# A two-block transformer kernel on one core: where ScalarE's function tables are asked for, and which set serves logarithm and exponential

## Time and profile before

| | |
|---|---|
| median of 3 runs | 3647.27 us (3642.99 to 3649.27) |
| the profiled execution | 3647.55 us |
| its span, first to last instruction | 3645.8 us |
| instructions | 48080 |
| mean granted TensorE clock | 0.92 of full |
| transfers | 325.77 MB, mean 89 GB/s |

### The profile page before, as it was taken

The page is one execution under the profiler, slowest core; times in us unless marked ns, Lnnn a source line. Parts: engine busy times, 40 slices in busy tenths (PEclk is TensorE's granted clock), DMA queues, the critical chain, the costliest instruction groups (busy, mean ns, idle before and its releaser), DMA issues.

```text
span 3645.8 us, 48080 instructions
## 1 busy us (share of the span) xinstructions
PE 3151.9 (86%) x19536; PEld 2419.4 (66%) x19536; DVE 1739.5 (48%) x2351; ACT 960.4 (26%) x1681; POOL 2018.1 (55%) x1184
## 2 busy tenths in 40 slices
PE   5996686699999677988999987988999998799997
PEld 4674464467776565766777766676777776688885
DVE  6724723334443443476666553185555564422233
ACT  3112112333332223122334323213233322200012
POOL 4812612344554553655666754573667674568773
PEclk9886697799999897999999998999999998899998
DMA  4332132211221243422222223432222222322321
GB/s 138 107 104 57 55 92 83 98 63 55 97 70 64 68 145 123 134 81 78 74 82 71 79 105 121 140 105 67 81 75 76 78 82 65 121 93 93 99 92 64
DMA packets 154796, 325.77 MB, mean 89 GB/s; under 512 B 34800, under 2 KB 71856, under 8 KB 154576
## 3 DMA queue, kind: packets, MB, share of 16 engines
q1 hardware_dynamic: 58752, 213.94, 18.1%
q10 hardware_dynamic: 95824, 108.76, 9.4%
HBM read 279.78 MB, written 42.86 MB: 88 GB/s over the span
## 4 chain that ended last, share of the span: by engine, by line
PE 71%; DVE 18%; ACT 4%; DMA 2%; ACTq 2%; issue 2%; POOL 0%; DVEq 0%
PE ps L1783 29%; PE ps L1824 11%; PE ps L1812 11%; PE ps L1637 2%; DVE acc_dense L2224 2%; DVE scan_tmp_vector L2224 2%; PE ps L1518 1%; DVE act_lo L2224 1%; PE ps L1548 1%; DVE ffh_lo L2915 1%; DVE rq L2224 1%; DVE added L2224 1%; PE ps L1558 1%; ACTq L960 1%; DVE xn_dense L2231 1%
## 5 line engine op out<-in xcount | busy, mean ns | idle before, releaser
L534 POOL TENSOR_TENSOR w_hi<-w_raw,ones 128x1024 fp32r<-128x1024 f32 x408 | 797.3, 1954 | 1256.6 <-DMA w_raw<-weights 1241.9
L536 POOL TENSOR_TENSOR w_lo<-w_raw,w_hi 128x1024 fp32r<-128x1024 f32 x408 | 1003.1, 2459 | 32.1
L1783 PE MATMUL ps<-act_hi,w_hi 128*128 128x512 f32 x1696 | 710.0, 419 | 6.6 <-DVE act_lo L2224 6.6
L1783 PE MATMUL ps<-act_lo,w_hi 128*128 128x512 f32 x1696 | 683.4, 403 | 0.0
L1783 PE MATMUL ps<-act_hi,w_lo 128*128 128x512 f32 x1696 | 679.2, 400 | 0.0
L1783 PEld LDWEIGHTS ps<-act_hi,w_hi 128*128 128x128 f32 x1696 | 327.4, 193 | 99.7 <-issue 16.5
L1783 PEld LDWEIGHTS ps<-act_hi,w_lo 128*128 128x128 f32 x1696 | 326.9, 193 | 76.3
L1783 PEld LDWEIGHTS ps<-act_lo,w_hi 128*128 128x128 f32 x1696 | 327.1, 193 | 67.5 <-issue 1.7
L2224 DVE TENSOR_TENSOR acc_dense<-acc_dense,ps 128x512 f32<-128x512 f32 x352 | 241.9, 687 | 236.5 <-PE ps L1812 176.5
L1812 PE MATMUL ps<-w_hi,ffh_hi 128*128 128x512 f32 x704 | 297.0, 422 | 54.5 <-DVE acc_dense L2224 51.0
L687 ACT ACT_TABLE_LOAD x204 | 261.7, 1283 | 258.0 <-PE ps L1783 104.2
(11 more groups left out here) (393 smaller groups left out, 4584.9 us busy)
## 6 DMA issues: line engine op xcount, KB each, us to landing
w_raw<-weights SPq DMA_DIRECT2D x408, 512.0 KB, 3.5
rw<-rw_t ACTq DMA_DIRECT2D x24, 256.0 KB, 2.3
rw<-lora_t ACTq DMA_DIRECT2D x24, 256.0 KB, 2.0
row<-x ACTq DMA_DIRECT2D x8, 512.0 KB, 3.5
row_dense<-x ACTq DMA_DIRECT2D x8, 512.0 KB, 3.6
res<-row_dense ACTq DMA_DIRECT2D x8, 512.0 KB, 2.6
row_mix<-res ACTq DMA_DIRECT2D x8, 512.0 KB, 7.6
res<-row_mix ACTq DMA_DIRECT2D x8, 512.0 KB, 2.9
```

The costliest lines, as they stand in the source:

```text
L534: pool.tensor_tensor(w_hi[:, s], raw, ones[:, 0:1].to_broadcast([P, 1024]), MUL).then_inc(w_hi_made, 1)
L536: pool.tensor_tensor(w_lo[:, s], raw, w_hi[:, s].bitcast(F32), SUB).then_inc(w_ready, 1)
L1783: mm = pe.matmul(out, ws[w][:, s, P * k:P * k + P], acts[a][:, k, x], start=(k, w, a) == (0, 0, 0), stop=(k, w, a) == (KT - 1, 1, 0))
```

## The change

A table `SETS` names one set per function; `Exp` and `Ln` both get `natural_log_exp_and_others`. A new helper `table_for` asks for a function's set if it isn't the one asked for last; ACT's order is fixed when the program is built, so the helper needs only one remembered name. All eight requests of before become calls of it, and a call is put in front of the waits of every step that uses a function with a table. `fn` asserts that the set is in. Nothing else changes: the same instructions with the same waits in the same order on all engines. The diff, cut:

```diff
+        SETS = {ACT.Exp: "natural_log_exp_and_others", ACT.Ln: "natural_log_exp_and_others", ACT.Silu: "silu_and_others",
+                ACT.Sigmoid: "sigmoid_and_others", ACT.Gelu: "gelu_and_others", ACT.Tanh: "exp_and_others", ACT.Sin: "trig_and_small"}
+        loaded = [""]
+
+        def table_for(func):
+            if loaded[0] != SETS[func]:
+                act.preload_act_table_set(SETS[func])
+                loaded[0] = SETS[func]
+
         def fn(out, in_, func, **kw):
+            assert func not in SETS or loaded[0] == SETS[func]
             return act.activation(out, in_, func, **kw)
...
         def exponent(h, u, br):
             v = HEAD_UNITS * h + u
+            table_for(ACT.Exp)
             if v >= 2 and br == 0:
                 act.wait_ge(at_psum, TURNS[v - 1])
...
                     if u and step == 2:
+                        table_for(ACT.Ln)
                         act.wait_ge(o_psum, v)
                         ss = small[:, 160 + (v - 1) % 2:161 + (v - 1) % 2]
                         give(fn(attn[h]["o_sq"][:, :], ps[:, 7, 0:VD], ACT.Square, accum_out=ss), act_step)
...
             yield
+            table_for(ACT.Gelu)
             act.wait_ge(y_landed, 16 * 32 * (h + 1))
...
             yield
+            table_for(ACT.Sigmoid)
             for m in range(4):
...
                 give(fn(sig[:, m], ps[:, glu_bank(h, m), :], ACT.Sigmoid, bias=glu_vec[:, m:m + 1]), glu_sig)
-            act.preload_act_table_set("natural_log_exp_and_others")
-            yield
+            table_for(ACT.Exp)
+            yield
+            table_for(ACT.Ln)
             take(glu_sum)
...
         def mix_norm(h):
             total = (acc_dense, acc_mix)[h]
             gx, gt_ = rows_before(1, h), turns_before(1, h)
-            act.preload_act_table_set("natural_log_exp_and_others")
+            table_for(ACT.Exp)
             for step in range(NORM_STEPS):
+                if step <= HALF:
+                    table_for(ACT.Ln)
                 if step < HALF:
...
                 give(fn(rw_t[:, n % 2], ps[:, 4 + n % 2, :], ACT.Copy, scale=rw_vec[:, 42 + m:43 + m]), rw_evac)
+                if n < 2:
+                    table_for((ACT.Tanh, ACT.Sigmoid)[n])
                 act.wait_ge(rw_mixed, N + 1)
...
                 act.wait_ge(lora_stored[q % 2], 16 * (6 * h + q // 2))
+            if kind < 2:
+                table_for(ACT.Sigmoid)
             act.wait_ge(lora_psum, Q + 1)
...
                 for k in range(HALF):
+                    if j == 3:
+                        table_for(ACT.Silu)
                     if k < HALF - 1:
                         act.wait_ge(tok_psum, (HALF - 1) * (4 * h + j) + k + 1)
...
                 yield
                 yield
+                table_for(ACT.Ln)
                 act.wait_ge(ret_var, i + 1)
...
         def rw_decays(v):
+            table_for(ACT.Exp)
             act.wait_ge(prep_dve, nth("p_dve", "arg", v))
...
         def rw_key_root(v):
+            table_for(ACT.Ln)
             act.wait_ge(prep_dve, nth("p_dve", "max", v))
...
         def rw_root(v):
+            table_for(ACT.Ln)
             act.wait_ge(rw_norm, nth("norm", "var", v))
...
                 if (kind, part) == ("gate", 3):
+                    table_for(ACT.Silu)
                     act.wait_ge(unit_done, AT[h, ff_unit(f, kind, m)] + 1)
...
         def dense_norm(c, h):
-            act.preload_act_table_set("natural_log_exp_and_others")
+            table_for(ACT.Exp)
             gx, gt = rows_before(c, h), turns_before(c, h)
...
             for step in range(NORM_STEPS):
                 if step < HALF:
+                    table_for(ACT.Ln)
                     if c == 3:
...
                         if uu == 3:
+                            table_for(ACT.Sigmoid)
                             if k < HALF - 1:
                                 act.wait_ge(gate_psum, (HALF - 1) * (2 * h + j) + k + 1)
```

More of the change, by code:

```diff
@@ L841, in ssm @@
         def ssm():
+            table_for(ACT.Exp)
             take(arg_ready)
             give(fn(wv[:, 1], wv[:, 1], ACT.Exp), fn_ready)
+            table_for(ACT.Sin)
             give(fn(wv[:, 3:5], wv[:, 3:5], ACT.Sin), fn_ready)
```

## The result

The changed kernel took 3622.96 us (median of 5 runs, 3611.72 to 3635.77) beside 3647.27 for the kernel before on the same chip (5 runs, 3642.65 to 3650.79): ratio 0.9937, 95% interval 0.9913 to 0.9962. Two more comparisons on other occasions gave 0.9931 and 0.9940. The mean of the three, 0.9936, is 23 us; forecast were 20.9 us and 3626.5.

The account below looks back on a forecast made before the run. TensorE, busy 3151.9 of 3645.8 us, was taken as the bound, so only loads on the chain count. Gains 12.83 + 5.9 + 1.85 + 0.30 = 20.9 us off 3647.3 gave 3626.5 us; range 3613 to 3640 (0.82).

Parts of the forecast that it names:

- the 31: Of 223 table loads, those the chain runs through, worth at most 39.8 us; 23 were to leave it, at most 29.5.
- the caps: Limits on each load's gain, taken from the idle time behind it that the trace shows; capped sum 20.9 us.
- Retention: Eight second loads between Ln and Exp vanish; DVE waited only 5.9 us for the root, against 10.3 us of loads: gain 5.9.
- rg_out: Loads at 1581.33 and 2443.06, moved ahead of waits; the rotation of rk holds PE, so gain 0 for both.
- 2161.26 and 2162.87: One load hidden ahead of a wait, one second load gone; DVE waited 1.85 us for the root: gain 1.85, not 2.57.
- 1175.79 and 1177.39: One load hidden, one gone, before one PE gap with almost only ACT's issuing of 32 transfers between: full gain of both.
- 1234.53: Load moved ahead of a long enough wait and hidden in full; the wait behind it is longer than the load: gain 1.283.
- 2644.70: Second load between Ln and Exp vanishes; PE's wait of 2.28 us at 2653.00 is longer than the load: gain 1.283.
- 1882.18: Second load between Ln and Exp vanishes; DVE's wait of 1.34 us at 1889.34 is longer than the load: gain 1.283.
- 1365.01: Request of L1013 for a set already in, skipped; PE's 13.85 us wait at 1378.14 is longer: gain 1.283.
- The drain: Rival: each switch also empties the engine, so a lost load frees twice its row: 33.7 us, 3613.6; chance 0.02.
- The clock: Rival: shifted PE gaps put more matmuls at TensorE's lower granted clock, making the kernel slower, 3655 us; chance 0.04.

Follow-up runs that it names:

- the two one-set kernels: Kernel before with Ln and Exp sharing one set: loads right in front of their functions, 0.9966; or waits in their old places, 0.9951, again 0.9943.
- the halves: Changed kernel with the combined set reloaded between Ln and Exp in four retention steps: first half only, 3631.4 us (0.9951); second half only, 3626.23 us (0.9933).
- the moves only: Changed kernel with Ln and Exp in separate sets and the old requests kept, loads still asked for ahead of the waits: 3645.41 us, ratio 1.0007.
- the reloaded kernel: Changed kernel with the combined set loaded once more between Ln and Exp in each of eight retention steps: 3638.8 us, ratio 0.998.
- the first four experiments: One set, loads right in front of functions (0.9966); moves with separate sets (1.0007); changed kernel again (0.9931); one load back per retention step (0.998).

## Why the prediction was right, and where its parts were not

- **How many loads stay; which are on the chain.** 146 and 861.7 us, as forecast. The chain of before has one load more than the 31, at 14.92 us, with 0.35 us on the chain; it is gone too, and the first matmul came 0.07 us earlier. That loads beside a busy PE cost nothing held: 45 put back cost 4 us, where six of them were thought to be on the chain (up to 7.3 us by the caps).
- **Retention, 5.9 us.** The wait is gone with the loads and comes back to the tenth with them. Its worth by time: 7 us between the two one-set kernels, 16 with all eight loads back (twice), 1.5 with the halves added. The cap is right for the wait; by time two of the three comparisons agree with it, and the 16 stays open. The traces say that the first half was worth more than its 3.2: matmuls 5600 to 6000 took 93.5 to 99.3 us in the six traces whose load stands in DVE's way there, and 89.3 to 91.0 in the eight others, 6 us apart in the mean. In the second half the spread (224.6 to 236.3 us for matmuls 11600 to 12800) hides what 2.7 us would do.
- **rg_out, 0.** The reason given, the rotation holding PE, holds in each trace looked at, to 0.1 us. The stretch of matmuls 4800 to 5600 was nevertheless 1.2 to 1.5 us shorter in the three traces of the changed kernel, by shorter rotations, and not in the four variants that kept the early load and were unaltered up to there (204.0 to 204.4, as before, 204.1); with the moves only it was 201.3. What sets that isn't shown.
- **1998.19, 0.30.** ACT stood 19.42 us ahead of the kernel before at the Ln, 20.70 at the Exp behind it, 19.80 three instructions later: 0.38 of 1.28 stayed.
- **2161.26 and 2162.87, 1.85 forecast.** Nothing stayed. DVE's wait of 1.85 us is gone, but the product behind it now took 2.37 us instead of 0.57:

```profile
2144.37 2.37 DVE L2752 TENSOR_TENSOR yn<-ys,small 128x256 f32<-128x256 f32 x1
```

  It started 0.29 us into GpSimd's w_lo, before 2.10 us into it, and in both kernels it ended 0.28 us behind that w_lo's end (2146.46 and 2164.77). DVE was 18.4 us ahead going in and 18.3 coming out.
- **1175.79 and 1177.39, 2.57 forecast.** This step of the forecast failed. It held that nearly nothing but ACT's own issuing lay between these loads and PE's gap. The changed kernel's time line:

```profile
1177.14 1.28 ACT L692 ACT_TABLE_LOAD   x1
1181.31 0.60 ACT L697 ACTIVATE ff_f<-ps 128x512 f32<-128x512 f32 x1 [2.88 <-PE ps L1819]
...
1182.10 16.50 ACTq L976 DMA_DIRECT2D y_raw<-y_scratch  x32
```

  Ahead of the 32 issues ACT waits for a matmul, now 2.88 us, before 0.31. Measured from o_sq (1175.40 and 1175.54), the issues begin 0.79 us earlier, not 2.57. The cap was taken from a gap of PE's further down the chain (9.67 us, up to 1201.73), and the nearest wait, ACT's own, was passed over.
- **1234.53, 1.28 forecast.** The sigmoid started 1.22 us earlier (1237.73 before, 1236.51 after), but Ln behind it only 0.38 (1248.80, 1248.42). Between them DVE does eight products; GpSimd's two splits came at the same time in both kernels (from 1238.03 and 1238.09 on). Before, the first two products met them (1.96 and 2.71 us); the earlier ones of the changed kernel left two unhindered and met them with the third and fourth:

```profile
1238.75 2.26 DVE L2260 TENSOR_TENSOR y_raw<-y_raw,sig 128x512 f32<-128x512 f32 x1
1241.05 2.71 DVE L2260 TENSOR_TENSOR ysq<-y_raw 128x512 f32<-128x512 f32 x1
```

  Of this gain and that of 1175 nothing reached the next norm: at ACT's last copy ahead of the load of 1365.01 the changed kernel was 0.32 us behind.
- **2644.70, 1.28 forecast.** 0.13 was left at ACT's zi_next behind it. PE's 2.28 us of waiting, from which I took the cap, is 2.28 us in the changed kernel too. What took the gain stands ahead of that gap. Before and changed:

```profile
2646.97 0.69 DVE L2915 TENSOR_TENSOR ffh_lo<-ff_f,ffh_hi 128x512 fp32r<-128x512 f32 x1 [2.58 <-ACT ffh_hi L687]
2623.74 1.85 DVE L2951 TENSOR_TENSOR ffh_lo<-ff_f,ffh_hi 128x512 fp32r<-128x512 f32 x1 [1.30 <-ACT ffh_hi L697]
```

  Against the work ahead of the load, ffh_lo came 1.28 us earlier, and it took 1.16 longer: it started 0.59 us into GpSimd's w_hi instead of 1.87. This is so in every trace: 1.85 us in the eleven without the load, 0.69 in the three with it. A gap of PE's was read as if ACT alone stood behind it.
- **1882.18, 1.28 forecast.** By ACT's own line 0.44 stayed (14.19 us ahead at the Exp, 13.35 at ffh_hi), because ACT waits for a matmul 0.8 us behind the Exp. The 4.5 us of that stretch come from ffh_lo's place against w_lo, as shown above, and not from this load: luck.
- **3011.15, 1.28 forecast.** ACT gained 0.63: a transfer that ACT issues ran beside this load, and the chain's row had shown 0.62 for it, not 1.28. The last 3100 matmuls took 637.5 and 637.3 us.
- **683.61, 1.28 forecast.** ACT ran 1.28 us earlier behind it; the 400 matmuls from number 2000 on took 153.7 and 153.1 us, 0.6 less.
- **1365.01, 1.28 forecast.** This one gave more than its length: 3.2 us. Matmul 4728, the first behind the load, came 1.16 us earlier, and the matmuls 4728 to 4800 took 33.5 and 31.5, 2.1 less. There DVE waits for a transfer, before and changed:

```profile
1384.42 1.28 DVE L2231 SCALAR_TENSOR_TENSOR acc_mix<-acc_mix,small,gain_post_dense 128x1024 f32<-128x1024 f32 x1 [4.98 <-DMA row_dense<-x]
1381.66 1.28 DVE L2267 SCALAR_TENSOR_TENSOR acc_mix<-acc_mix,small,gain_post_dense 128x1024 f32<-128x1024 f32 x1 [3.05 <-DMA row_dense<-x]
```

  It repeats: matmuls 4727 to 4800 took 44.5 to 45.1 us in the twelve traces that skip this request, and 47.8 and 48.0 in the two that make it (before, and moved only). Why the transfer came 1.9 us sooner isn't shown.
- **2245.62 and 2272.77, 1.28 each.** Between 2251 and 2294 us ACT gained 4.9 us on the kernel before (18.3 us ahead, then 23.2); at the end of the stretch (matmul 11600) 2.9 were left, in the other two traces of the changed kernel 9.8 and -0.1.
- **The moves.** Forecast 4.4 us (three of 1.28 and 0.56). The changed kernel stands at 0.9936, one set without moves at 0.9947: 4 us, give or take 6. Alone they gave -3 us, give or take 7, and what they are worth stays open. One set and the skipped requests gave 19 us of the 23; the caps had 16.5.
- **The drain.** Ln, load and Exp run with 0.02 us between them in the reloaded kernel too, and the gain is under the 33.7 us of that rival. The trace bears out the 1283 ns of the Trainium skill, "ScalarE: Activation LUTs", section "What ACT_TABLE_LOAD costs", and not its further 1.38 us.
- **The clock.** The mean stayed at 0.92; the rival from that side was wrong. But its mechanism works in the small, in both directions: 0.86 to 0.84 in the first stretch of the result, 0.90 to 0.96 in the second.

So the total is right partly by luck: errors cancelled. The loads at 1175 to 1235 gave nothing that lasted (3.85 forecast), 2161 nothing (1.85), 2644 and 3011 together 0.8 of 2.57. The request at 1365, the first retention and the stretch behind it gave about 2, 5 and 4.5 more than forecast. The rule that held is that loads off the chain cost nothing that can be measured. A cap was no bound: the places one by one were known to no better than some 2 us, and the first retention by less. The step that failed most often is the same: an engine's idle time further down was taken as what a load frees, without asking what else starts between the load and that gap.

## What to carry to other kernels

Logarithm and exponential in one loop belong in the one table set that serves both, and the load belongs ahead of the wait; but look where it stands in the compiled kernel first, since a request written directly in front of the function can push it behind a wait that the compiled one already ran under. Count loads on the chain, not in the page, and cap each by the first wait behind it, on its own engine too, not by a gap further down. If VectorE works on SBUF operands beside a GpSimd that does so as well, don't expect a gain of a microsecond to arrive as a microsecond: look where the earlier VectorE product will start, ahead of GpSimd's instruction or inside it. Repeat the run before explaining a difference of a few microseconds.

## What the runs showed of the hardware that was not expected

**A VectorE product with both inputs in SBUF that starts inside a GpSimd split ends just behind the split.** The changed kernel by tile (fastest, median, slowest in ns; first and last start):

```profile
L2260 DVE TENSOR_TENSOR acc_dense<-acc_dense,ps x352: 686/687/691, 843.5 to 3530.7; 128x512 f32<-128x512 f32 x176
L2951 DVE TENSOR_TENSOR ffh_lo<-ff_f,ffh_hi x88: 691/988/2843, 750.0 to 3510.7; 128x512 fp32r<-128x512 f32 x88
```

Same shape, same operation. acc_dense, with one input in PSUM, took 686 to 691 ns all 352 times, though GpSimd was at w_lo or w_hi at the start of 142 of them. Of ffh_lo, 38 started outside the splits and took 0.71 us in the mean; 50 started inside, mean 1.54, up to 2.84, four times the shortest. Of these 50, 49 ended 0.55 us behind the end of the split in which they had started, wherever in it that was; so what is gained in front of such a product is lost in it, as long as it starts in the same split. In each trace 98 to 113 of VectorE's 2351 instructions were over 1 us longer than the same instruction in the best of the traces, 175 to 198 us in all, mostly off the path. The Trainium skill, "SBUF — State Buffer", section "Who interferes with whom", says that a VectorE instruction with two SBUF inputs contends with a GpSimd instruction that reads SBUF, and that one with at most one SBUF input does not. These rows agree; the change's forecast left it out, and at 1234, 1882, 2161 and 2644 it is what scattered its parts.

**Much of the spread between executions goes with TensorE's granted clock, in stretches that the edits don't touch.** The two kernels with the loads in one half are alike up to the first retention, and their first 4180 matmuls took, in the order of first and second half:

```profile
23.16:1187.96 1164.80, 972.09 (x4181) 714.48 (x4181) 512.19 (x816) 275.99 (x581) 506.48 (x347) 0.86 0.25 79
```

```profile
23.15:1171.16 1148.01, 953.28 (x4181) 700.58 (x4181) 510.52 (x816) 275.64 (x580) 506.51 (x347) 0.88 0.26 80
```

17 us apart: PE's busy time is 18.8 us longer at a mean of 0.86 than at 0.88, its idle time 2 us shorter. Over the 29 executions of the kernel before beside the first four experiments, time and mean clock move together too (correlation -0.90). What sets the clock there isn't shown. The 17 us are three quarters of the whole effect under study, and the reason why the comparisons can't settle 4 us.
